# Four modulation chunks of the second layer on GpSimd, and a new order of loads, modulation pieces and start

## Chip, cores and metric

The kernel runs on one core of one Trainium2 chip. The metric is device time in microseconds (us) of one execution, the median of several. All data are float32.

## What is computed

A first block of two layers over 256 tokens of width 2048, and behind it a second block of one layer (two-way scans over tokens and context, then a mixture of 16384 small experts). What this change touches is the input projection of the first block's layers and the second block's modulation:

```python
for i in range(DEPTH):                       # first block, DEPTH = 2
    u = rms_norm(h, norm_g[i]); z = u @ w_in[i]
    ...                                      # three kinds of attention -> mixed
    h = h + mixed @ w_o[i]
    h = h + (p[i] @ w_ple[i]) * jax.nn.sigmoid(h @ w_pg[i])
...
# second block
sh1, sc1, gt1, sh2, sc2, gt2 = split(silu(c) @ w_ada + b_ada, 6)
csh1, csc1, cgt1, ...        = split(silu(c_ctx) @ w_ada + b_ada, 6)
```

Of the modulation of the context only the first two of six parts (shift and scale before its projection) are used. `silu(c) @ w_ada` is a row of 12288 numbers, made in 24 chunks of 512.

## The kernel before

**Weight stream.** All large weights lie in one DRAM tensor `stream` of chunks (2048 x 512), each cut into four pieces: four blocks of 128 rows, laid out as 128 x 2048, 1 MB. SyncE's queue loads the pieces in the fixed order `RING` (made by `layer_order`) into the four buffers of `ring`, round robin; a load waits until the buffer's last piece is used (`piece_used`, L886). To keep float32 precision at TensorE's faster rate, each main piece is split into two: ScalarE rounds it to `high` (`split`, L1846) and VectorE subtracts, `ring - high`, into `ring_r` (L2460). TensorE multiplies with both (`product`, three matmuls of 512 columns, L301 to L303), for two tiles of 128 tokens and four blocks: 24 matmuls a piece (`products`).

**Slots.** A layer has 88 slots, one main piece each: 56 of the input projection, 16 of the output projection, 16 of the gate. After the products of slot q every engine does its share of side work for that slot (`side(l, q)`: norms, rope, heads, attention, turns), so the program order on each engine is written out by hand. In slots 14 to 77 ScalarE and VectorE do side work first and then the split of that slot, elsewhere the split first. Slots 60 and 61 share their products.

**Modulation pieces.** Seven modulation chunks lie in each of the two layers, four pieces each, at the slots listed in `ADA_SLOTS`: the piece follows the main piece of that slot in the ring. It isn't split: TensorE multiplies it directly in float32 with two columns, `silu(c)` and `silu(c_ctx)` (`ada_pe`, L350). After the fourth piece ScalarE copies the four partial rows from PSUM to `mod_rows` (`ada_act`, L366), at the slot after the chunk's last TensorE turns and sums them to columns (`ada_turn`, L357), and VectorE keeps them in `adac` (`ada_dve`, L371).

**Large loads.** GpSimd issues them in its own order, behind waits for their places: `w_uq` and `w_ukv` (L955, L956) once the tiles of `x` are split, the residual (2 MB, L959) when all heads are done, in the second layer then `trig`, `b_ada`, the context in four parts (L964) and `final_g` (L966), then `w_ple` (2 MB) and `pT` (L969, L970) after slot 69. At the end of the second layer it stores the residual in quarters (L979), each behind `gate_used`, which VectorE signals in `use_gate(l, e)` at slot 78 + 4e.

**Beginning.** SyncE loads `cols`, `wtail`, `bc`, `positions`, `inv_freq`, `lam`, then `x` in four parts, then the ring. VectorE makes the rotary angles, ScalarE their sines; TensorE turns `x` (`turn_x`, L1049, L1050), ScalarE rounds it (`round_x`, L1853), VectorE makes the low halves (`split_x`, L2467); then slots 0 to 2 are split and multiplied.

Of the kernel before, what the change touches and what calls it, by code (L numbers as in the profile page):

```python
# [26 lines left out]
ALU = mybir.AluOpType  # L27
# [137 lines left out]
def build_program(nc, t):  # L165
    ctx = ExitStack()
    with ctx:
# [65 lines left out]
        consts = sem("consts")  # L233
# [294 lines left out]
        EXP_FIRST = SIDE_FIRST  # L528

# [342 lines left out]
        def _(sp):  # L872

            sp.dma_start(cols[:, :], t["cols"]).then_inc(consts, 16)
            sp.dma_start(wsmall[:, 0:256], t["wtail"]).then_inc(consts, 16)
            sp.dma_start(bc[:, :], t["bc"].partition_broadcast(P)).then_inc(consts, 16)
# [3 lines left out]
            for e in range(4):  # L880
                sp.dma_start(hx[:, :, e * CHUNK:(e + 1) * CHUNK], t["x"][:, e * CHUNK:(e + 1) * CHUNK].rearrange("(t p) d -> p t d", p=P))\
                  .then_inc(x_loaded[e], 16)
            for c, j, b, u in RING:
                if u >= 1:
                    sp.wait_ge(piece_used[b], u)
                sp.dma_start(ring[:, b, :], t["stream"][c, j]).then_inc(piece_full[b], 16)  # L886
# [52 lines left out]
        def _(pool):  # L939
            for n, (name, l) in enumerate(STAGES):  # L940
# [8 lines left out]
                elif name == "layers":  # L949
                    for l in range(DEPTH):  # L950
# [88 lines left out]
        def _(pe):  # L1039
# [3 lines left out]
            for n, (name, l) in enumerate(STAGES):  # L1043
                begin(pe, n, () if name in FLOWING or name == "peer" else ALL)
                if name == "layers":
# [17 lines left out]
                    def head_groups(l, r):  # L1063

                        if r == 0:
                            pe.wait_ge(turn_read["act"], TURN_ACT(l, "ta", 1))
                            pe.wait_ge(turn_read["dve"], TURN_DVE(l, "ta", 2))
                            pe.wait_ge(layer_loads, 48 * l + 32)
# [141 lines left out]
                    def embed(l, i):  # L1210

                        e, s = i // 2, i % 2
                        if i == 0:
# [7 lines left out]
                    def side(l, q):  # L1221
# [44 lines left out]
                        elif q == 50:  # L1266
# [3 lines left out]
                            pe.wait_ge(ada_done, ADA_LAYER * l + 5)  # L1270
# [72 lines left out]
                    for e in range(4):  # L1343
                        pe.wait_ge(x_loaded[e], 16)
                        turn_x(e, (2 * e, 2 * e + 1))
# [492 lines left out]
        def _(sc):  # L1838
            for n, (name, l) in enumerate(STAGES):
                begin(sc, n, () if name in FLOWING else ALL)  # L1840
                if name == "layers":
# [133 lines left out]
                    def side(l, q):  # L1975
# [110 lines left out]
                        for a0, slots in enumerate(ADA_SLOTS):  # L2086
                            if q == slots[-1] + 2:
                                ada_act(sc, ADA_LAYER * l + a0)

                    sc.wait_ge(consts, 16 * 3)  # L2090
                    sc.activation(cols[:, C_SILU:C_SILU + 2 * KT], cols[:, C_SILU:C_SILU + 2 * KT], ACT.Silu)
                    sc.wait_ge(trig_made, 1)
                    sc.activation(trig[:, 1, :, :], zs[:, 128:192].rearrange("p (t n) -> p t n", t=NT), ACT.Sin)
                    sc.activation(trig[:, 0, :, :], zs[:, 192:256].rearrange("p (t n) -> p t n", t=NT), ACT.Sin)
                    sc.activation(st[:, 64:68], st[:, 68:72], ACT.Exp).then_inc(lam_exp, 1)
                    for e in range(4):
                        round_x(0, e, (2 * e, 2 * e + 1))
                    sc.copy(tail_high, wtail[:, 0]).then_inc(tail_made, 1)
                    for q in range(3):
                        split(0, q)  # L2100
                    for e in range(4):
                        sc.wait_ge(x_loaded[e], 16)
                        square_x(hx, e)
                    sc.drain().then_inc(x_square, 1)
                    for l in range(DEPTH):
                        for q in range(SLOTS):
                            if (l or q >= 3) and q not in EXP_FIRST:
                                split(l, q)
                            if l:
# [326 lines left out]
        def _(dve):  # L2436
# [12 lines left out]
            for n, (name, l) in enumerate(STAGES):  # L2449
# [5 lines left out]
                elif name == "layers":  # L2455
# [196 lines left out]
                    def add_out(l, n4):  # L2652

                        if n4 == 0:
                            dve.wait_ge(layer_loads, 48 * (l + 1))
# [189 lines left out]
                    dve.wait_ge(small, 16 * 3)  # L2845
                    pos, inv = st[:, 80:82], zs[:, 0:32]
                    chain(dve, "dve", dve.tensor_copy(pos, sti[:, 0:NT]))
                    for s in range(NT):
                        a = dve.tensor_scalar(zs[:, 32 + s * 32:64 + s * 32], inv, pos[:, s:s + 1], None, ALU.mult)
                    chain(dve, "dve", a)  # L2850
                    ang, turns, r = zs[:, 32:96], zs[:, 96:160], zs[:, 128:192]
                    turns = zs[:, 256:320]

                    chain(dve, "dve", dve.tensor_scalar(turns, ang, float(np.float32(1 / TWO_PI)), 12582912.0, ALU.mult, ALU.add))
                    chain(dve, "dve", dve.tensor_scalar(turns, turns, 12582912.0, None, ALU.subtract))
                    c1 = 6.28125
                    c2 = float(np.float32(np.round((TWO_PI - c1) * 2 ** 20) / 2 ** 20))
                    c3 = float(np.float32(TWO_PI - c1 - c2))
                    prev = ang
# [788 lines left out]
```

## Time and profile before

| | us |
|---|---|
| median of 3 runs | 3770.86 (3768.49 to 3772.71) |
| profiled execution | 3777.06 |
| its span | 3775.5 |
| TensorE matmul busy | 3712.3 (98%) |
| VectorE busy | 2363.9 (63%) |
| ScalarE busy | 1571.1 (42%) |
| GpSimd busy | 109.2 (3%) |
| mean granted TensorE clock | 0.994 |

The profiled execution is one run with the hardware profiler; its span is the time from the first to the last recorded instruction. Busy shares are averages over the whole span; matmul ends are modelled, so 98% is the share of time with matmuls in flight and not the share of TensorE's peak. Granted clock 1 is the upper level of TensorE's clock. The two layers take the first 1290 us of the span.

### The profile page before, as it was taken

The numbers are of one execution on the slowest core, as the hardware profiler recorded it, in microseconds if no ns is written. First come the engines' busy times: TensorE is split into PE (matmuls) and PEld (weight loads), VectorE is DVE, ScalarE is ACT, GpSimd is POOL, SyncE is SP. The second block draws the span as 40 slices with busy tenths as digits, with TensorE's granted clock in tenths as the row PEclk, the third lists the DMA queues.
The fourth block names the chain that finished last, engine by engine and source line by source line (L and its number), as shares of the span: only waits on it lengthen the run. The fifth ranks groups of instructions, "written<-read, shape, count | busy, mean of one in ns | idle before, by whom it ended". The sixth has DMA issues, their size and how long they took to land.

```text
span 3775.5 us, 48150 instructions
## 1 busy us (share of the span) xinstructions
PE 3712.3 (98%) x20154; PEld 3127.5 (83%) x20154; DVE 2363.9 (63%) x3164; ACT 1571.1 (42%) x1559; POOL 109.2 (3%) x147
## 2 busy tenths in 40 slices
PE   7999999999999999999999999999999999999998
PEld 6777877777777778988888799999988888888886
DVE  4456644436645767665746589777566666667877
ACT  4344535334444521255543433355433333333333
POOL 0000000000000000020000000000000000000000
PEclk9999999999999999999999999999999999999999
DMA  6545565745565467543466445556666666666664
GB/s 247 185 170 221 208 229 189 265 156 206 212 245 211 163 241 283 212 178 126 149 213 258 169 168 191 205 208 235 227 240 228 228 222 222 222 245 234 236 248 173
DMA packets 118857, 799.34 MB, mean 212 GB/s; under 512 B 13264, under 2 KB 13648, under 8 KB 31120
## 3 DMA queue, kind: packets, MB, share of 16 engines
q1 hardware_dynamic: 96992, 692.73, 51.3%
q0 software_dynamic: 19376, 82.96, 5.7%
q10 hardware_dynamic: 2304, 20.97, 1.3%
q8 instruction: 142, 2.33, 0.2%
q14 instruction: 43, 0.35, 0.0%
HBM read 752.57 MB, written 44.04 MB: 211 GB/s over the span
## 4 chain that ended last, share of the span: by engine, by line
PE 91%; DVE 3%; DMA 3%; ACT 2%; POOL 1%; issue 0%; SPq 0%; DVEq 0%; POOLq 0%; ACTq 0%
PE ps L301 25%; PE ps L303 24%; PE ps L302 24%; PE ps L1771 5%; DMA ring<-in_stream_dram 3%; PE ps L1773 2%; PE ps L1723 2%; DVE ring_r L2460 1%; PE ps L350 1%; ACT high L1846 1%; PE ps L1218 1%; PE ps L1082 1%; PE ps L1562 1%; DVE ring_r L315 1%; PE ps L1511 0%; PE ps L1050 0%
## 5 line engine op out<-in xcount | busy, mean ns | idle before, releaser
L309 ACT CAST high<-ring 128x2048 fp32r<-128x2048 f32 x384 | 733.7, 1912 | 1191.9 <-DMA ring<-in_stream_dram 1187.1
L315 DVE TENSOR_TENSOR ring_r<-ring,high 128x2048 fp32r<-128x2048 f32 x384 | 880.1, 2293 | 539.3 <-ACT high L309 537.2
L303 PE MATMUL ps<-high,act_r 128*128 128x512 f32 x1952 | 763.5, 391 | 0.0
L301 PE MATMUL ps<-high,z_r 128*128 128x512 f32 x1728 | 678.9, 393 | 2.8 <-DVE z L3475 1.3
L302 PE MATMUL ps<-ring_r,z_r 128*128 128x512 f32 x1728 | 673.5, 390 | 0.0
L301 PE MATMUL ps<-high,h_r 128*128 128x512 f32 x1600 | 643.7, 402 | 21.4 <-DVE ring_r L2460 17.8
L2460 DVE TENSOR_TENSOR ring_r<-ring,high 128x2048 fp32r<-128x2048 f32 x176 | 402.5, 2291 | 379.8 <-ACT high L1846 378.1
L302 PE MATMUL ps<-ring_r,h_r 128*128 128x512 f32 x1600 | 625.6, 391 | 0.0
L303 PE MATMUL ps<-high,z_r 128*128 128x512 f32 x1376 | 535.9, 389 | 0.0
L302 PE MATMUL ps<-act_r,high 128*128 128x256 f32 x1664 | 471.7, 283 | 0.0
L1846 ACT CAST high<-ring 128x2048 fp32r<-128x2048 f32 x176 | 334.5, 1911 | 279.6 <-DMA ring<-in_stream_dram 278.9
L303 PEld LDWEIGHTS ps<-high,act_r 128*128 128x128 f32 x1952 | 367.9, 188 | 79.3
L301 PE MATMUL ps<-act_r,high 128*128 128x256 f32 x1472 | 420.7, 286 | 2.4 <-DVE act_r L3331 2.4
L303 PE MATMUL ps<-act_r,ring_r 128*128 128x256 f32 x1472 | 417.4, 284 | 0.0
L301 PEld LDWEIGHTS ps<-high,h_r 128*128 128x128 f32 x1600 | 301.3, 188 | 131.7 <-issue 48.6
L301 PEld LDWEIGHTS ps<-high,z_r 128*128 128x128 f32 x1728 | 324.9, 188 | 82.4 <-issue 14.8
L302 PEld LDWEIGHTS ps<-ring_r,z_r 128*128 128x128 f32 x1728 | 325.1, 188 | 67.2 <-issue 1.0
L302 PEld LDWEIGHTS ps<-ring_r,h_r 128*128 128x128 f32 x1600 | 301.6, 189 | 58.2 <-issue 0.7
L302 PEld LDWEIGHTS ps<-act_r,high 128*128 128x128 f32 x1664 | 320.0, 192 | 0.0
L303 PEld LDWEIGHTS ps<-high,z_r 128*128 128x128 f32 x1376 | 258.3, 188 | 54.5
L1771 PE MATMUL ps<-act_r,high 128*128 128x512 f32 x832 | 294.8, 398 | 0.0
L301 PEld LDWEIGHTS ps<-act_r,high 128*128 128x128 f32 x1472 | 283.1, 192 | 2.5 <-issue 2.5
(509 smaller groups left out, 3968.5 us busy)
## 6 DMA issues: line engine op xcount, KB each, us to landing
ring<-in_stream_dram SPq DMA_DIRECT2D x656, 1024.0 KB, 4.8
hidden<-z POOLq DMA_DIRECT2D x32, 512.0 KB, 6.4
gate_matrix<-z ACTq DMA_DIRECT2D x8, 2048.0 KB, 7.0
r<-gate_matrix POOLq DMA_DIRECT2D x32, 512.0 KB, 6.4
z<-hidden POOLq DMA_DIRECT2D x32, 512.0 KB, 6.8
r<-in_w_ple_dram POOLq DMA_DIRECT2D x2, 2048.0 KB, 9.4
merge_gates<-r ACTq DMA_DIRECT2D x8, 512.0 KB, 5.1
r<-merge_gates POOLq DMA_DIRECT2D x4, 1024.0 KB, 5.9
```

Source lines behind the costliest of these rows:

```text
L301: pe.matmul(out, lhs[0], rhs[0], start=start, stop=False)
L302: pe.matmul(out, lhs[0], rhs[1], start=False, stop=False)
L303: return pe.matmul(out, lhs[1], rhs[0], start=False, stop=stop)
L309: sc.copy(high[:, j, :], ring[:, j, :]).then_inc(piece_high[j], 1)
L315: dve.tensor_tensor(ring_r[:, j, :], ring[:, j, :], high[:, j, :], ALU.subtract).then_inc(piece_low[j], 1)
L350: mm = pe.matmul(ps[32 * q:32 * q + 2, 7, :], cols[:, C_SILU + 2 * k:C_SILU + 2 * k + 2], ring[:, b, q * CHUNK:(q + 1) * CHUNK], start=(j ...
L1082: mm = pe.matmul(ps[:, bank, (hd % 2) * TOK:(hd % 2 + 1) * TOK], w[:, k, hd * HD:(hd + 1) * HD], src[:, k, :], start=(k == 0), stop=(k == ...
L1723: mm = pe.matmul(ps[:, 4 + t // 4 % 4, (t % 4) * P:(t % 4 + 1) * P], hot1[:, k % HOTS, t % 8, :], hot2[:, k % HOTS, t % 8, :], start=True, ...
L1771: mm = pe.matmul(ps[:, b, :].rearrange("p (s n) -> p s n", s=2), w[0], halves_2(k), start=(k == 0), stop=(k == KT - 1))
L1773: mm = pe.matmul(ps[:, b, TOK:], w[1], high_2(k), start=False, stop=False)
L1846: sc.copy(high[:, b, :], ring[:, b, :]).then_inc(piece_high[b], 1)
L2460: dve.tensor_tensor(ring_r[:, b, :], ring[:, b, :], high[:, b, :], ALU.subtract).then_inc(piece_low[b], 1)
```

## The change

Four modulation chunks of the second layer (8, 11, 12 and 13, `ADA_POOL`) are multiplied and summed on GpSimd: for each block of 128 rows the 128 x 512 weights times the column `silu(c)`, added to `mod_rows`. The turn on TensorE then also sums over the partitions (a product with a column of ones). Only the token's modulation is made, not the context's. The places of all modulation pieces change. `w_uq` is loaded in three parts, `w_ple` in four, and these and the context's parts stand behind waits for given slots. At the beginning `x` parts and the first pieces alternate in SyncE's queue, the first parts of `x` are processed between the first slots, and angles and squares come in slots 3 to 7.

```diff
-ADA_SLOTS = ((5, 8, 9, 11), (14, 15, 16, 17), (28, 30, 31, 32), (35, 36, 37, 38), (41, 43, 44, 45), (57, 59, 61, 63), (76, 78, 80, 83))
+ADA_SLOTS = ((3, 5, 7, 9), (12, 14, 16, 18), (28, 30, 32, 34), (38, 40, 42, 44), (59, 61, 63, 65), (68, 70, 72, 74), (77, 79, 81, 83))
+ADA_POOL = (8, 11, 12, 13)
...
+        def ada_pool(pool, a, j):
+
+            b, u = A_AT[a, j]
+            if j == 0:
+                pool.wait_ge(ada_turned, a)
+            pool.wait_ge(piece_full[b], 16 * (u + 1))
+            for q in range(PIECE_KT):
+                k = PIECE_KT * j + q
+                w, c = ring[:, b, q * CHUNK:(q + 1) * CHUNK], cols[:, C_SILU + 2 * k:C_SILU + 2 * k + 1]
+                if k == 0:
+                    o = pool.tensor_scalar(mod_rows, w, c, None, ALU.mult)
+                else:
+                    chain(pool, "pool", pool.tensor_scalar(w, w, c, None, ALU.mult))
+                    o = pool.tensor_tensor(mod_rows, mod_rows, w, ALU.add)
+                if q < PIECE_KT - 1:
+                    chain(pool, "pool", o)
+            o.then_inc(piece_used[b], 1)
+            pool.wait_ge(piece_used[b], u + 1)
+            if j == 3:
+                pool.drain().then_inc(ada_rows, 1)
+
...
+            if a in ADA_POOL:
+                pe.wait_ge(ada_done, a)
+                for b in range(4):
+                    mm = pe.matmul(ps[:, 7, 2 * b:2 * b + 1], mod_rows[:, b * P:(b + 1) * P], ones[:, 0:1], start=True, stop=True)
+                mm.then_inc(ada_turned, 1)
+                return
...
+            if a in ADA_POOL:
+                dve.tensor_copy(adac[:, 4 * a:4 * a + 4, 0], ps[:, 7, 0:8:2]).then_inc(ada_done, 1)
+                return
...
+            sp.dma_start(cols[:, :], t["cols"]).then_inc(x_loaded[0], 16)
+            sp.dma_start(wsmall[:, 0:256], t["wtail"]).then_inc(x_loaded[0], 16)
+            load_x(0)
+            load_piece(*RING[0])
+            load_x(1)
+            load_piece(*RING[1])
+            load_x(2)
+            load_piece(*RING[2])
+            load_x(3)
+            load_piece(*RING[3])
...
+            sp.dma_start(bc[:, :], t["bc"].partition_broadcast(P)).then_inc(small, 16)
+            for piece in RING[4:]:
+                load_piece(*piece)
...
-                        pool.dma_start(w_uq, t["w_uq"][l].rearrange("(k p) n -> p k n", p=P)).then_inc(layer_loads, 16)
+                        for k in range(3):
+                            if k:
+                                b, u, _ = W_AT[l, 2 * k]
+                                pool.wait_ge(piece_used[b], u + 1)
+                            pool.dma_start(w_uq[:, k, :], t["w_uq"][l][k * P:(k + 1) * P, :]).then_inc(layer_loads, 16)
+                        b, u, _ = W_AT[l, 6]
+                        pool.wait_ge(piece_used[b], u + 1)
                         pool.dma_start(w_ukv, t["w_ukv"][l].rearrange("(k p) n -> p k n", p=P)).then_inc(layer_loads, 16)
+                        if l + 1 == DEPTH:
+                            for j in range(4):
+                                ada_pool(pool, 8, j)
                         pool.wait_ge(at_out, HEADS * (l + 1))
                         pool.wait_ge(at_done, HEADS * (l + 1))
                         pool.dma_start(hx_of[l], (HRES if l else t["x"]).rearrange("(t p) d -> p t d", p=P)).then_inc(layer_loads, 16)
...
                             pool.dma_start(trig[:, :, :, :], t["trig2"]).then_inc(consts_p, 16)
                             pool.dma_start(b_ada, t["b_ada"]).then_inc(consts_p, 16)
                             for e in range(4):
+                                b, u, _ = W_AT[l, (57, 59, 61, 63)[e]]
+                                pool.wait_ge(piece_used[b], u + 1)
+                                if e:
+                                    ada_pool(pool, 11, e - 1)
                                 pool.dma_start(crows[:, :, e, :], t["ctx"][:, e * CHUNK:(e + 1) * CHUNK].rearrange("(t p) d -> p t d", p=P)).then_inc(consts_p, 16)
+                            ada_pool(pool, 11, 3)
                             pool.wait_ge(tile_full, TILES(l, "mixed", 9))
                             pool.dma_start(final_g, t["final_g"].partition_broadcast(P)).then_inc(aux, 16)
+                            ada_pool(pool, 12, 0)
                         b, u, _ = W_AT[l, OUT_SLOT + OUT_PIECES.index((3, 1))]
                         pool.wait_ge(piece_used[b], u + 1)
-                        pool.dma_start(w_ple, t["w_ple"][l].rearrange("(k p) n -> p k n", p=P)).then_inc(ple_loaded, 16)
                         pool.dma_start(pT, t["pT"][l].rearrange("(k p) n -> p k n", p=P)).then_inc(ple_loaded, 16)
+                        for e in range(4):
+                            cs = slice(e * CHUNK, (e + 1) * CHUNK)
+                            if e:
+                                if l + 1 == DEPTH:
+                                    ada_pool(pool, 12, e)
+                                b, u, _ = W_AT[l, (71, 73, 76)[e - 1]]
+                                pool.wait_ge(piece_used[b], u + 1)
+                                pool.wait_ge(ple_loaded, 80 * l + 16 * (e + 1))
+                            pool.dma_start(w_ple[:, :, cs], t["w_ple"][l][:, cs].rearrange("(k p) n -> p k n", p=P)).then_inc(ple_loaded, 16)
                         if l + 1 < DEPTH:
                             pool.wait_ge(gate_used, 4 * (l + 1))
                             pool.dma_start(HRES.rearrange("(t p) d -> p t d", p=P), hx).then_inc(h_spilled, 16)
                     for e in range(4):
+                        ada_pool(pool, 13, e)
...
-                            pe.wait_ge(ple_loaded, 32 * (l + 1))
-                        else:
+                        if s == 0:
+                            pe.wait_ge(ple_loaded, 80 * l + 32 + 16 * e)
+                        if i:
...
+                    def turn_first_x(e):
+
+                        pe.wait_ge(x_loaded[e], 48 if e == 0 else 16)
+                        if e == 3:
+                            pe.wait_ge(tile_low, TILES(0, "x", 4))
+                        turn_x(e, X_BANKS[e])
+
+                    turn_first_x(0)
+                    turn_first_x(1)
                     for l in range(DEPTH):
                         for q in range(SLOTS):
+                            if l == 0 and q == 3:
+                                pe.wait_ge(tile_low, TILES(0, "x", 8))
                             for p, blocks in parts_of(q):
                                 products(l, p, blocks)
+                            if l == 0 and q < 2:
+                                turn_first_x(2 + q)
...
-                                    elif q == 57:
+                                    elif q == 59:
                                         pe.wait_ge(tile_low, TILES(l, "mixed", 5))
-                                    ada_pe(pe, a, slots.index(q))
+                                    if a not in ADA_POOL:
+                                        ada_pe(pe, a, slots.index(q))
```

ScalarE's and VectorE's orders at the beginning change accordingly: `round_x(0, e)` and `split_x(0, e)` alternate with `split(0, e)`; the squares of `x` come at slots 3 and 4, the angles at slots 4 (VectorE) and 6 (ScalarE); an early `Silu` on `ones` comes ahead of the first wait.

## Rows read from the trace of the kernel before

**Rows 1.** The page's first part: span, busy time and share of each engine, instructions.

```profile
span 3775.5 us, 48150 instructions
...
PE 3712.3 (98%) x20154; PEld 3127.5 (83%) x20154; DVE 2363.9 (63%) x3164; ACT 1571.1 (42%) x1559; POOL 109.2 (3%) x147
```

**Rows 2.** Waits of TensorE, 0 to 1400 us: us in total, times, longest.

```profile
PE ps L301 <- DVE ring_r L2460: 22.7, 19, 9.0
PE ps L1049 <- DMA act<-in_x_dram: 9.4, 1, 9.4
```

**Rows 3.** Stretches: length; PE, PEld, DVE, ACT, POOL busy (instructions); PEclk; DMA share; GB/s.

```profile
23.30:29.80 6.50, 6.42 (x19) 4.68 (x20) 4.90 (x7) 6.28 (x16) 0.00 (x0) 0.54 0.00 0
...
1103.90:1107.90 4.00, 3.99 (x11) 3.14 (x12) 3.59 (x4) 1.25 (x1) 0.00 (x0) 0.57 1.02 429
```

**Rows 4.** Timeline of the beginning: start us, us, engine, line, operation.

```profile
3.81 2.47 SPq L881 DMA_DIRECT2D act<-in_x_dram  x4
...
9.40 0.45 PE L1049 MATMUL ps<-ident,act 128*128 128x128 f32 x1 [9.40 <-DMA act<-in_x_dram]
```

**Rows 5.** The chain of waits, the beginning: start us, us, what.

```profile
19.12 1.81 ACT high L1846
20.95 2.30 DVE ring_r L2460
23.38 0.76 PE ps L301
```

**Rows 6.** The chain of waits: one piece that TensorE waited for, slot 8.

```profile
82.30 4.80 DMA ring<-in_stream_dram
87.12 1.92 ACT high L1846
89.06 2.30 DVE ring_r L2460
```

**Rows 7.** The chain of waits, slots 83 and 84 of the second layer.

```profile
1265.79 0.97 PE ps L350 x8
1266.76 0.43 PE ps L301
...
1272.47 0.79 PE ps L357 x8
```

**Rows 8.** The chain of waits: the piece beside the large loads.

```profile
1087.81 11.71 DMA ring<-in_stream_dram
```

**Rows 9.** Groups of GpSimd's instructions by shape: busy us, mean ns, idle before.

```profile
L388 POOL TENSOR_TENSOR z<-z,trig 128x512 f32<-128x512 f32 x1 | 1.3, 1297 | 0.0
...
L944 POOL TENSOR_SCALAR_AFFINE_SELECT ident<-ident 128x128 f32<-128x128 f32 x1 | 0.3, 295 | 0.2 <-POOL ident L943 0.2
```

**Rows 10.** Timeline of GpSimd, 1640 to 1680 us (the rope of the scan).

```profile
1650.33 2.32 POOL L386 TENSOR_TENSOR act<-z,trig 128x512 f32<-128x512 f32 x1
...
1659.21 1.28 POOL L389 TENSOR_TENSOR act<-z,trig 128x512 f32<-128x512 f32 x1
...
1661.82 3.35 POOL L391 TENSOR_TENSOR z<-act 128x512 f32<-128x512 f32 x1
1665.45 1.29 POOL L386 TENSOR_TENSOR z<-z,trig 128x512 f32<-128x512 f32 x1 [0.29 <-POOL z L391]
```

**Rows 11.** Timeline of VectorE in the same stretch.

```profile
1651.71 3.09 DVE L315 TENSOR_TENSOR ring_r<-ring,high 128x2048 fp32r<-128x2048 f32 x1 [0.21 <-ACT high L309]
...
1661.58 2.43 DVE L315 TENSOR_TENSOR ring_r<-ring,high 128x2048 fp32r<-128x2048 f32 x1
```

**Rows 12.** Timeline of VectorE, 1240 to 1300 us (gate quarters, pieces).

```profile
1246.24 1.29 DVE L2684 TENSOR_TENSOR act<-z 128x512 f32<-128x512 f32 x2
...
1256.50 2.29 DVE L2460 TENSOR_TENSOR ring_r<-ring,high 128x2048 fp32r<-128x2048 f32 x1 [1.66 <-ACT high L1846]
...
1277.37 1.29 DVE L2684 TENSOR_TENSOR act<-z 128x512 f32<-128x512 f32 x2
```

**Rows 13.** Timeline of GpSimd, 1060 to 1300 us: the third store.

```profile
1278.96 0.73 POOL L979 DMA_DIRECT2D residual<-act  x1 [30.39 <-DVE act L2684]
```

More of the change, by code:

```diff
@@ L2086, in side, with angles @@
                         for a0, slots in enumerate(ADA_SLOTS):
-                            if q == slots[-1] + 2:
+                            if q == slots[-1] + 2 and ADA_LAYER * l + a0 not in ADA_POOL:
                                 ada_act(sc, ADA_LAYER * l + a0)
-                    sc.wait_ge(consts, 16 * 3)
+                    sc.activation(rs[:, 90:91], ones[:, 0:1], ACT.Silu)
+                    sc.wait_ge(x_loaded[0], 48)
                     sc.activation(cols[:, C_SILU:C_SILU + 2 * KT], cols[:, C_SILU:C_SILU + 2 * KT], ACT.Silu)
[L2092 to L2095, printed above, removed]
-                    for e in range(4):
[L2097 to L2104, printed above, removed]
+                    def angles():
+                        sc.wait_ge(trig_made, 1)
+                        sc.activation(trig[:, 1, :, :], zs[:, 128:192].rearrange("p (t n) -> p t n", t=NT), ACT.Sin)
+                        sc.activation(trig[:, 0, :, :], zs[:, 192:256].rearrange("p (t n) -> p t n", t=NT), ACT.Sin)
+                        sc.activation(st[:, 64:68], st[:, 68:72], ACT.Exp).then_inc(lam_exp, 1)
+                    for e in range(4):
+                        round_x(0, e, X_BANKS[e])
+                        if e == 0:
+                            sc.copy(tail_high, wtail[:, 0]).then_inc(tail_made, 1)
+                        if e < 3:
+                            split(0, e)
                     for l in range(DEPTH):
@@ L2108, in _ @@
                                 split(l, q)
+                            if l == 0 and q in (3, 4):
+                                for e in (2 * q - 6, 2 * q - 5):
+                                    sc.wait_ge(x_loaded[e], 48 if e == 0 else 16)
+                                    square_x(hx, e)
+                                if q == 4:
+                                    sc.drain().then_inc(x_square, 1)
+                            elif l == 0 and q == 6:
+                                angles()
                             if l:
@@ L2844, in _ @@
                     dve.tensor_reduce(sel16[:, :], ident[:, :].rearrange("p (q s) -> p s q", q=4)[:, 0:16, :], AX_X, ALU.add)
[L2845 to L2858, printed above, removed]
@@ L2859, in _ @@
-                    prev = ang
-                    for cc in (c1, c2, c3):
-                        chain(dve, "dve", dve.scalar_tensor_tensor(r, turns, -cc, prev, ALU.mult, ALU.add))
-                        prev = r
-                    pi = float(np.nextafter(np.float32(np.pi), np.float32(0)))
-                    chain(dve, "dve", dve.tensor_scalar(r, r, pi, -pi, ALU.min, ALU.max))
-                    c = zs[:, 192:256]
-                    chain(dve, "dve", dve.scalar_tensor_tensor(c, r, -1.0, r, ALU.mult, ALU.max))
@@ L2886, in _, with angles @@
-                    chain(dve, "dve", dve.tensor_tensor(st[:, 60:62], e[:, :, 1], e[:, :, 0], ALU.subtract))
-                    for ly in range(DEPTH):
-                        init = 0.8 - 0.6 * float(np.exp(-0.3 * ly))
-                        dve.tensor_scalar(st[:, 60 + ly:61 + ly], st[:, 60 + ly:61 + ly], -init, None, ALU.add)
-                        dve.tensor_scalar(bc[:, B_SUB + ly * HD:][:, 0:HD], bc[:, B_SUB + ly * HD:][:, 0:HD], 1.0 - init, None, ALU.mult)
+                    def angles():
+                        dve.wait_ge(small, 16 * 4)
+                        pos, inv = st[:, 80:82], zs[:, 0:32]
+                        chain(dve, "dve", dve.tensor_copy(pos, sti[:, 0:NT]))
+                        for s in range(NT):
+                            a = dve.tensor_scalar(zs[:, 32 + s * 32:64 + s * 32], inv, pos[:, s:s + 1], None, ALU.mult)
+                        chain(dve, "dve", a)
+                        ang, turns, r = zs[:, 32:96], zs[:, 96:160], zs[:, 128:192]
+                        turns = zs[:, 256:320]
+                        chain(dve, "dve", dve.tensor_scalar(turns, ang, float(np.float32(1 / TWO_PI)), 12582912.0, ALU.mult, ALU.add))
+                        chain(dve, "dve", dve.tensor_scalar(turns, turns, 12582912.0, None, ALU.subtract))
+                        c1 = 6.28125
+                        c2 = float(np.float32(np.round((TWO_PI - c1) * 2 ** 20) / 2 ** 20))
+                        c3 = float(np.float32(TWO_PI - c1 - c2))
+                        prev = ang
+                        for cc in (c1, c2, c3):
+                            chain(dve, "dve", dve.scalar_tensor_tensor(r, turns, -cc, prev, ALU.mult, ALU.add))
+                            prev = r
+                        pi = float(np.nextafter(np.float32(np.pi), np.float32(0)))
+                        chain(dve, "dve", dve.tensor_scalar(r, r, pi, -pi, ALU.min, ALU.max))
+                        c = zs[:, 192:256]
+                        chain(dve, "dve", dve.scalar_tensor_tensor(c, r, -1.0, r, ALU.mult, ALU.max))
+                        dve.tensor_scalar(c, c, -1.0, float(np.float32(np.pi / 2)), ALU.mult, ALU.add)
+                        lam = zs[:, 512:1024].rearrange("p (k l n) -> p k l n", k=4, l=DEPTH)
+                        for ly in range(DEPTH):
+                            for pr in range(2):
+                                k = 2 * ly + pr
+                                dve.tensor_tensor_reduce(zs[:, 1024 + k * 64:][:, 0:64], lam[:, 2 * pr, ly, :], lam[:, 2 * pr + 1, ly, :],
+                                                         1.0, 0.0, ALU.mult, ALU.add, st[:, 68 + k:69 + k])
+                        dve.drain().then_inc(trig_made, 1)
@@ new lines, in factors @@
+                    def factors():
+                        dve.wait_ge(lam_exp, 1)
+                        e = st[:, 64:68].rearrange("p (l k) -> p l k", k=2)
+                        chain(dve, "dve", dve.tensor_tensor(st[:, 60:62], e[:, :, 1], e[:, :, 0], ALU.subtract))
+                        for ly in range(DEPTH):
+                            init = 0.8 - 0.6 * float(np.exp(-0.3 * ly))
+                            dve.tensor_scalar(st[:, 60 + ly:61 + ly], st[:, 60 + ly:61 + ly], -init, None, ALU.add)
+                            dve.tensor_scalar(bc[:, B_SUB + ly * HD:][:, 0:HD], bc[:, B_SUB + ly * HD:][:, 0:HD], 1.0 - init, None, ALU.mult)
@@ L2891, in _ @@
+                    dve.wait_ge(x_loaded[0], 48)
+                    for e in range(4):
+                        split_x(0, e, X_BANKS[e])
+                        if e == 0:
+                            dve.wait_ge(tail_made, 1)
+                            dve.tensor_tensor(tail_low, wtail[:, 0], tail_high, ALU.subtract).then_inc(tail_made, 1)
+                        if e < 3:
+                            split(0, e)
                     for l in range(DEPTH):
@@ L2894, in _ @@
                                 split(l, q)
+                            if l == 0 and q == 4:
+                                angles()
+                            elif l == 0 and q == 7:
+                                factors()
                             if l:
```

47 lines of the change are left out of this document (12 added, 35 removed).

## Prediction

> **What bounds the kernel now.** I read the page's first part first: TensorE is busy for 98% of the span [rows 1], so time comes only out of TensorE's own work or out of its idle time, and anything that another engine does matters only when TensorE ends up waiting for it. Next the waits of TensorE over the two layers [rows 2]. The reader is to see that there is little to win by better timing: 9.4 us for the first part of `x`, and 22.7 us for the halves of weight pieces, of which one wait at the start is 9.0 and the other eighteen share 13.7. Then the stretches right behind an idle time [rows 3]: after the 9.0 us wait the granted clock is 0.54 for 6.5 us, and after a wait of 3.0 us it is 0.57 for 4.0 us. Those are the lower of TensorE's two levels, and they cost 3.0 us and 1.7 us beside the waits themselves. Last, the chain of waits, which shows what a late piece goes through: load 4.80, cast on ScalarE 1.92, subtraction on VectorE 2.30 [rows 6], 9.1 us with the hand-overs, of which TensorE then makes 24 products in about 5.5 us (from 1266.76 to 1272.47 at slot 84, less the slow first product [rows 7]).
>
> The SyncE queue issues the pieces strictly in ring order, four buffers deep. A piece of slot q is called Mq here, a modulation piece that follows it Aq. With modulation pieces at every second slot the buffer of Aq is next used by M(q+3), since M(q+1), M(q+2) and A(q+2) lie between. So M(q+3) is ready 9.1 us after Aq is used, and TensorE wants it when M(q+2) is finished.
>
> **Gains.** (1) *Start.* `x` is issued behind six small or broadcast loads and its first part lands at 9.40, 5.6 us after the issue at 3.81 [rows 4]. Four parts of it are then turned and rounded before the first piece is cast at 19.12, subtracted until 23.25 and multiplied from 23.38 [rows 5]. In the changed kernel the first part of `x` is third in the queue (issue about 1.9, landing about 7.0 to 7.5). ScalarE rounds one part (four operations, 1.5 us), casts the piece to 12, VectorE subtracts to 14.3: the first product starts 9.1 us earlier. Two parts are turned between slots 0 to 2 instead of in the idle time, 16 transposes of 0.11 us, 1.8 us in all. The later slots have their halves in time by the same reckoning (slot 3's at about 37 against a start at 38), and the angles and squares fall into slots 3 to 7, behind pieces already loaded. Net 7.3, between 5 and 10. (2) *Sixteen pieces off TensorE.* Each takes 0.97 us, and the product behind it 0.43 where 0.23 is usual [rows 7]: 16 x 1.17 = 18.7 us (15.5 without the second part). The turn of each chunk stays (0.79 us). (3) *Places.* The clusters with modulation pieces at adjoining slots leave less than 9.1 us; most of the 13.7 us lies there and behind large loads. Every second slot leaves two main pieces and one modulation piece, 11.9 us. I take 8 (3 to 12), clock losses included. (4) *Large loads in parts.* The 3.0 us wait comes after a piece that took 11.71 us to land [rows 8], beside the residual and context loads. The 2 MB residual load is still issued whole just ahead. I take 3 (0 to 6). Gains: 7.3 + 18.7 + 8 + 3 = 37; bounds 24 and 47.
>
> **What a piece costs on GpSimd.** There are four multiplications by a scalar and four additions, 128x512 each, every one chained to the last. A two-input operation of that form takes 1.30 us undisturbed [rows 9]. The one-input form is not in the trace: by scaling the selection of 128x128 with its fixed part taken as a 0.2 us memset's it is about 0.57, and it will not cost more than the two-input form's 1.30. I take 0.7, near the one-input row. With about 0.1 us for each chained wait: 4 x 1.30 + 4 x 0.7 + 0.8 = 8.8 us; a chunk's first piece has one addition less, 7.3 us with its missing wait. Bounds alone are 8.0 and 11.
>
> Alone it is not. While VectorE subtracts a 128x2048 piece, GpSimd's 1.3 us operations take 2.32 to 3.35 us; the later one began 0.24 us behind VectorE's 2.43 us subtraction and lasted 2.06 us beyond its usual time [rows 10, 11]. So GpSimd stands still for nearly the whole of such a subtraction, and VectorE loses little: 3.09 for 2.29 at worst. In a stretch where TensorE finishes two main pieces there are two subtractions, 4 us: 12.8 us for a piece, 11.2 for a first one (one subtraction and the gating products of slot 59). Bounds are 8.0 (no overlap) and 16.
>
> The Trainium skill speaks against this move: "GPSIMD Engine Reference", section Engine selection, keeps elementwise work on VectorE, puts two-input operations on GpSimd at about twice the time and one-input ones near line rate, and its Key points say that GpSimd shares its SBUF interfaces with VectorE when that has two SBUF inputs. The trace agrees on the sharing. At line rate for the one-input operations (an estimate from the page: 512 columns at 1.2 GHz, 0.43 us) a piece would take 7.7 us alone instead of 8.8, and the sum below would be some 5 us better.
>
> **What holds the pieces up.** *Chunk 8* (slots 12 to 18). GpSimd can start a piece as it lands, and slots 14 to 17 also carry the query and key products of the heads, so M15, M17, M19 and M21 have over 12 us to spare for A. Nothing. *Chunk 11* (59 to 65). GpSimd waits until TensorE has used M59 before it starts A59, and M61 before A61, M63 before A63 (the order written there serves the context loads). Take M59's end as 0. A59 is done at 11.2, M62 ready at 20.3; TensorE is through M60 and M61 at 12.1: a stall of 8.2, and 3 us at the low clock. A61 runs 12.8 to 25.6, M64 is ready at 34.7 against 34.3: 0.4. A63 starts at M63's end and is done at 47.8, M66 ready at 56.9 against 46.5: 10.4, and 3 of clock. Together 25; with pieces of 8.0 it is 13, with 16 it is 31. A65 then just suffices for the turn at slot 66. *Chunk 12* (68 to 74). A70 starts 1.5 us behind M69's end (two DMA issues), so M73 is ready at 1.5 + 12.8 + 9.1 = 23.4 against 17.3: 6.1, and 3 of clock, 9; bounds 1 and 12. *Chunk 13* (77 to 83). Each piece stands behind the wait and the store for a quarter of the residual. The second quarter is released by VectorE at 1247.5, the third at 1278.7, when the store is issued (1278.96) [rows 12, 13]. So A81 runs from 1248.3 to 1261.1, M84 is ready at 1270.2 against 1265.8: 4.4. M84's subtraction ended at 1258.8 before [rows 12]; 11 us later, with M85 and M86 and the third quarter behind it in VectorE's order, that quarter comes some 7 us later. A83 cannot start before 1286 and ends at 1295 (VectorE now waits too, so 8.8). But TensorE wants the whole chunk at slot 84's end, where its turn is at 1272.47 [rows 7]: it comes 22.6 us late. Clock 3. Together 26 (4.4 is inside the 22.6); with 8.0 us and M84 in time 1279.3 + 8.0 - 1272.5 + 3 = 18; upper 30. What is late next is the key and value stage, which starts that much later: it is bound by TensorE itself and gives nothing back.
>
> **Sum.** Losses 25 + 9 + 26 = 60 (bounds 32 and 73), gains 37 (24 and 47): 23 us slower. The profiled execution took 3777.06 (span 3775.5 and 1.6 around it), 6.2 above the median of the three runs, so from it the changed kernel takes 3800; the same difference on the median gives 3770.9 + 23 = 3794 us.
>
> **Rivals.** *A, the pieces are cheap* (the other side): if the subtractions don't hold GpSimd and a piece takes about 8, losses are 32 and gains 37 to 47: 3756 to 3766. Point of decision: losses under 30. For it speaks that most of rows 10 in the second rope half run at 1.29; against it the waits at M59, M63 and the third quarter, which stand however short a piece is. *B, hidden and paid back*: losses about equal to gains, pieces near 9.5, within 7.5 us of 3771. *C, contention above my value*: in the first rope half six operations took 14.8 us instead of 7.8, a factor of 1.9. At 16 us a piece losses are 73 and the time is 3771 + 36 = 3807, with the smallest gains 3820. *D, the start does not move*, because the loads are limited by bandwidth: 3801, inside the range. *E*, only the last turn stalls and chunks 11 and 12 run free (if my reading of their waits is wrong): 26 against 37, 3760.
>
> **Chances.** Forecast with C and D 0.68 (slower), B 0.13 (same), A and E 0.19 (faster); 0.2% is 7.5 us, about what this kernel's measurement can tell from nothing. The range runs from 3758 (A and E's better half left out) to 3816 (C's worst left out); the forecast's own is 3780 to 3812.
>
> **What the profile would show.** First product near 14.3; 320 instead of 448 records for line 350's matmuls; GpSimd some 200 us busier, its additions 1.3 or 3.3; TensorE waits of 6 to 10 us for M62, M66 and M73, and one of about 16 at the turn behind slot 84, released by GpSimd, each followed by a stretch at the low clock. I am wrong if GpSimd's pieces are finished before TensorE has used the two main pieces behind them, or if the third quarter is released much earlier than slot 84's end.

## The result

The changed kernel takes 3825.1 us in the median (3821.5 to 3827.2, 4 runs) against 3771.8 for the kernel before beside it: a ratio of 1.0141, 95% interval 1.0128 to 1.0155, so 53 us slower. The direction was forecast, the size was not: 3794 was predicted and 3816 was the end of the range.

The profile after, first part and shares of the chain that ended last. The line numbers have moved (L1846 is now L1925, L2460 is L2548, L1049 is L1117, L1218 is L1286, L357 is L380 for the chunks on GpSimd).

```profile
span 3820.0 us, 48041 instructions
...
PE 3701.5 (97%) x20026; PEld 3131.0 (82%) x20026; DVE 2382.0 (62%) x3164; ACT 1565.8 (41%) x1546; POOL 338.9 (9%) x281
...
PE 88%; POOL 4%; DVE 3%; DMA 2%; ACT 1%; issue 1%; POOLq 0%; DVEq 0%; SPq 0%; ACTq 0%
```

TensorE is busy for 11 us less than in [rows 1] and the span is 44.5 us longer; GpSimd is 230 us busier and now has a share of the chain. The waits of TensorE, 0 to 1500 us (total, times, longest), answer to [rows 2]:

```profile
PE ps L301 <- DVE ring_r L2548: 44.1, 17, 9.3
PE ps L380 <- POOLq L373: 21.0, 3, 20.1
PE ps L1286 <- ACT z L2139: 12.7, 1, 12.7
PE ps L1117 <- DMA act<-in_x_dram: 8.3, 2, 6.6
```

All long ones but the 6.6 us for the first part of `x` lie behind the heads of the second layer. The beginning, by contrast, did what it should. In its timeline the first part of `x` is there at 6.57 and the first product comes at 13.84, 9.5 us before that of [rows 5]:

```profile
6.57 0.45 PE L1117 MATMUL ps<-ident,act 128*128 128x128 f32 x1 [6.57 <-DMA act<-in_x_dram]
...
13.84 0.77 PE L301 MATMUL ps<-high,h_r 128*128 128x512 f32 x1 [1.59 <-DVE ring_r L2548]
```

GpSimd's groups by shape (busy us, mean ns, idle before) show the price that [rows 9] did not hold:

```profile
L366 POOL TENSOR_SCALAR ring<-ring,cols 128x512 f32<-128x512 f32 x60 | 119.4, 1991 | 19.0 <-DMA ring<-in_stream_dram 9.5 <-PE ps L303 4.4
L367 POOL TENSOR_TENSOR wsmall<-wsmall,ring 128x512 f32<-128x512 f32 x60 | 95.2, 1587 | 5.0
```

The one-input multiplication is dearer than the two-input addition. Undisturbed it is 1.56 against 1.26 to 1.30, as the timeline of GpSimd for A61 shows, and beside VectorE's subtractions 3.48:

```profile
1088.96 1.56 POOL L366 TENSOR_SCALAR ring<-ring,cols 128x512 f32<-128x512 f32 x1 [0.34 <-PE ps L303]
1090.60 1.26 POOL L367 TENSOR_TENSOR wsmall<-wsmall,ring 128x512 f32<-128x512 f32 x1
...
1094.96 3.48 POOL L366 TENSOR_SCALAR ring<-ring,cols 128x512 f32<-128x512 f32 x1
...
1099.90 3.48 POOL L366 TENSOR_SCALAR ring<-ring,cols 128x512 f32<-128x512 f32 x1
1103.46 1.29 POOL L367 TENSOR_TENSOR wsmall<-wsmall,ring 128x512 f32<-128x512 f32 x1
```

A61 begins 0.34 us behind TensorE's use of M61 and ends at 1104.75 (1103.46 + 1.29), after 15.8 us. VectorE's own rows in that stretch are the subtractions of M62 and M63:

```profile
1094.32 2.69 DVE L2548 TENSOR_TENSOR ring_r<-ring,high 128x2048 fp32r<-128x2048 f32 x1 [13.99 <-ACT high L1925]
1098.64 3.30 DVE L2548 TENSOR_TENSOR ring_r<-ring,high 128x2048 fp32r<-128x2048 f32 x1 [1.63 <-ACT high L1925]
```

And this is what TensorE did meanwhile, M62, M64 and M66 in its timeline of chunk 11, and M73 in chunk 12:

```profile
1097.15 0.77 PE L301 MATMUL ps<-high,z_r 128*128 128x512 f32 x1 [8.31 <-DVE ring_r L2548]
...
1113.91 0.77 PE L301 MATMUL ps<-high,r_r 128*128 128x512 f32 x1 [4.18 <-DVE ring_r L2548]
...
1134.58 0.80 PE L301 MATMUL ps<-high,z_r 128*128 128x512 f32 x1 [7.08 <-DVE ring_r L2548]
```

```profile
1188.69 0.76 PE L301 MATMUL ps<-high,h_r 128*128 128x512 f32 x1 [9.31 <-DVE ring_r L2548]
```

The last chunk holds the largest losses. First GpSimd (second store, A81, third store, A83), which answers to [rows 13]:

```profile
1266.21 0.78 POOL L1047 DMA_DIRECT2D residual<-act  x1 [13.79 <-DVE act L2772]
1267.04 2.25 POOL L366 TENSOR_SCALAR ring<-ring,cols 128x512 f32<-128x512 f32 x1
...
1279.28 1.26 POOL L367 TENSOR_TENSOR wsmall<-wsmall,ring 128x512 f32<-128x512 f32 x1
1304.72 0.77 POOL L1047 DMA_DIRECT2D residual<-act  x1 [24.18 <-DVE act L2772]
1305.53 1.57 POOL L366 TENSOR_SCALAR ring<-ring,cols 128x512 f32<-128x512 f32 x1
...
1316.20 1.26 POOL L367 TENSOR_TENSOR wsmall<-wsmall,ring 128x512 f32<-128x512 f32 x1
```

Then ScalarE and TensorE in the same stretch:

```profile
1285.27 1.90 ACT L1925 CAST high<-ring 128x2048 fp32r<-128x2048 f32 x1 [20.98 <-DMA ring<-in_stream_dram]
1287.07 0.58 ACT L2139 COPY z<-ps 128x512 f32<-128x512 f32 x1
```

```profile
1287.70 3.76 PE L1286 MATMUL ps<-r 128*128 128x512 f32 x4 [12.70 <-ACT z L2139]
...
1317.91 1.87 PE L380 MATMUL ps<-ones,wsmall 128*128 128x1 f32 x8 [20.09 <-POOLq L373]
```

ScalarE's program has the cast of M84 ahead of the copy of an embedding product. M84's load waits for A81, so ScalarE sits 21 us, and TensorE, which needs that copy's bank already at slot 83, stops there for 12.7 us. The wait that names ScalarE is GpSimd's. Behind it comes the forecast one: A83 stands behind the third store, and the turn behind slot 84 waits 20.1 us. Two stretches (columns as in [rows 3]) show the lower level of the clock behind that wait, 0.54, and the mean over the 270 us from the heads to the last turn, 0.87:

```profile
1318.00:1326.00 8.00, 8.00 (x24) 6.65 (x25) 0.39 (x2) 1.90 (x1) 0.60 (x1) 0.54 0.72 281
```

```profile
1060.00:1330.00 270.00, 199.45 (x827) 155.26 (x826) 121.75 (x107) 90.98 (x100) 179.34 (x109) 0.87 0.50 193
```

### The profile page after: what moved, and what is told of

The parts are those of the page before. It is cut to its first block, busy times and chain, and to the rows that moved or that the text cites. A ratio compares the mean times of both kernels' runs of the same rounds, so it can differ in the third digit from the quotient of the medians.

```text
span 3820.0 us, 48041 instructions
## 1 busy us (share of the span) xinstructions
PE 3701.5 (97%) x20026; PEld 3131.0 (82%) x20026; DVE 2382.0 (62%) x3164; ACT 1565.8 (41%) x1546; POOL 338.9 (9%) x281
## 4 chain that ended last, share of the span: by engine, by line
PE 88%; POOL 4%; DVE 3%; DMA 2%; ACT 1%; issue 1%; POOLq 0%; DVEq 0%; SPq 0%; ACTq 0%
PE ps L301 24%; PE ps L303 23%; PE ps L302 23%; PE ps L1850 5%; PE ps L1852 2%; DMA ring<-in_stream_dram 2%; POOL ring L366 2%; PE ps L1802 1%; POOL wsmall L367 1%; PE ps L350 1%; DVE ring_r L2548 1%; PE ps L1150 1%; PE ps L1641 1%; DVE ring_r L315 1%; ACT high L1925 0%
## 5 line engine op out<-in xcount | busy, mean ns | idle before, releaser
L2548 DVE TENSOR_TENSOR ring_r<-ring,high 128x2048 fp32r<-128x2048 f32 x176 | 409.5, 2327 | 382.4 <-ACT high L1925 381.1
L1925 ACT CAST high<-ring 128x2048 fp32r<-128x2048 f32 x176 | 335.3, 1910 | 336.1 <-DMA ring<-in_stream_dram 335.2
```

The source lines that it names most:

```text
L1925: sc.copy(high[:, b, :], ring[:, b, :]).then_inc(piece_high[b], 1)
L2548: dve.tensor_tensor(ring_r[:, b, :], ring[:, b, :], high[:, b, :], ALU.subtract).then_inc(piece_low[b], 1)
```

## Experiments

(In the kernels here line numbers are up to 3 higher or lower than in the changed one.) All runs compare with the kernel before on the same chip; its median was 3772.2 to 3773.0. The 95% intervals are 4 to 6 us to either side, so a difference of less than some 5 us between two kernels is not clear of noise. "Theory 1" is that GpSimd's long pieces hold the ring's buffers, "theory 2" that GpSimd costs in proportion to its busy time, "theory 3" that the new places or beginning carry part of the loss.

**Which part loses.** `ADA_POOL` sets which chunks GpSimd makes; a chunk that is not in it goes back to TensorE at its new place.

```diff
-ADA_POOL = (8, 11, 12, 13)
+ADA_POOL = ()             # pool_none;  (8,) pool_8;  (8, 11) pool_8_11;  (8, 13) pool_8_13;  (8, 12) pool_8_12
         def ada_pool(pool, a, j):
             b, u = A_AT[a, j]
+            if a not in ADA_POOL:
+                return
```

No chunk on GpSimd. 

> The changed kernel with no chunk on GpSimd: all four go back to TensorE, at their new places; beginning, places and parts of loads as changed. Theory 1 (the loss is the ring held up by GpSimd's pieces of about 16 us, and the rest of the change is the gain I took it for: 7 at the start, 8 by places, 3 by loads): 3754 us. Theory 2 (GpSimd's work costs in proportion to its busy time, by slowing VectorE, wherever it lies): the same 3754. Theory 3 (the new places or the new beginning carry part of the loss): 3772 or more.

Measured 3759.3 us, ratio 0.9963 (0.9949 to 0.9977). Theory 3 falls: the rest of the change gains 13 us. It is 5 less than the 18 expected, but the interval (9 to 19 us) holds the 18 too.

Chunk 8 alone. 

> As above, but chunk 8 (slots 12 to 18, beside the heads' projections) on GpSimd. Theory 1: hidden, four pieces off TensorE at 1.17 us, 5 us faster than without any: 3749. Theory 2: a quarter of the whole loss of some 71 us: 3771.

Measured 3754.6, ratio 0.9954 (0.9937 to 0.9970), the fastest kernel here. The medians differ by 4.7 from the run above, the four pieces' worth that was forecast (4 x 1.17), though the two intervals overlap. Theory 2 falls: four pieces of 13.3 to 15.0 us on GpSimd, from 719 to 786 us, cost nothing visible. Around them TensorE is busy without a gap at the upper clock (1.00), in this run (first line) as in the one with nothing on GpSimd (second line; columns as in [rows 3]):

```profile
700.00:850.00 150.00, 150.00 (x697) 119.66 (x698) 74.34 (x118) 59.65 (x81) 54.74 (x31) 1.00 0.48 178
700.00:850.00 150.00, 150.00 (x709) 116.07 (x709) 65.90 (x109) 58.92 (x80) 0.00 (x0) 1.00 0.49 178
```

Chunks 8 and 11. 

> Chunks 8 and 11 on GpSimd. Theory 1: the waits of TensorE in chunk 11 of the changed kernel (8.3 + 1.5 + 4.2 + 7.1 = 21 us) and some 8 us of low clock, less 5 for the pieces: 24 us slower than with chunk 8 alone, 3773. Theory 2: as for every chunk, about 18 slower.

Measured 3775.0, ratio 1.0010 (1.0001 to 1.0020): 20.4 us above chunk 8 alone. This run by itself doesn't part theory 1 (24) from theory 2 (18).

Chunks 8 and 13. 

> Chunks 8 and 13 on GpSimd. Theory 1: the waits 2.9 + 12.7 + 20.1 = 36 us of the changed kernel and some 8 us of low clock, less 5: 39 us slower than with chunk 8 alone, 3788; a few less if the lateness of A77 came from chunk 12. Theory 2: about 18 slower, 3767 to 3789.

Measured 3790.8, ratio 1.0048 (1.0032 to 1.0065): 36.2 above. The chunks cost very different amounts for the same work. Its waits are the same two as in the changed kernel, so they belong to chunk 13 and not to what came before it:

```profile
PE ps L382 <- POOLq L375: 21.1, 1, 21.1
PE ps L301 <- DVE ring_r L2550: 12.9, 13, 2.4
PE ps L1288 <- ACT z L2141: 12.4, 1, 12.4
```

Chunks 8 and 12. 

> Chunks 8 and 12 on GpSimd. If the chunks' costs add up, chunk 12 costs what is left of the changed kernel's loss: 3825 - 3755 - 20 (chunk 11) - 36 (chunk 13) = 14, so 3769. If the three in a row make each other worse: less, 3762 to 3766.

Measured 3764.7, ratio 0.9973 (0.9963 to 0.9983): 10.1 above chunk 8 alone, in the second range. The three chunks singly add 20.4 + 10.1 + 36.2 = 66.7 and together 70.5, so nearly all of the loss is the sum of the single ones. The 4 us that are left are within the noise; whether standing in a row adds anything is not settled.

**When a piece starts.** In the next two, pieces are moved ahead of the waits that stand before them in GpSimd's order.

```diff
                     for e in range(4):
                         ada_pool(pool, 13, e)
+                    for e in range(4):
                         if e == 3:
```

> Chunks 8 and 13 on GpSimd as in the run before, but all four pieces of chunk 13 ahead of the residual's stores in GpSimd's order, so that none waits for a gate quarter. Theory 1 (the start behind those waits is what delays them): the pieces follow each other from slot 76's end, 15 to 16 us each; M82 and M84 are late by 2 us each at most, the turn at slot 84 by 0 to 2: 3753 to 3758, so 33 to 38 faster than with the waits (3791). Theory 4 (the pieces are too long for their places wherever they start): three further pieces behind a first, each 16 against 14.5 us of TensorE's work between them, and the low clock: 3765 or more.

Measured 3756.5, ratio 0.9960 (0.9946 to 0.9974): 34.3 us faster than with the waits, and 1.9 above chunk 8 alone. The same work, 15.4 us a piece here, now costs almost nothing, so theory 4 falls for this chunk. Its waits from 1180 to 1290 us, where there had been 36:

```profile
PE ps L301 <- DVE ring_r L2551: 4.1, 3, 1.4
PE ps L382 <- POOLq L375: 1.5, 1, 1.5
```

```diff
                             for e in range(4):
+                                if e:
+                                    ada_pool(pool, 11, e - 1)
                                 b, u, _ = W_AT[l, (57, 59, 61, 63)[e]]
                                 pool.wait_ge(piece_used[b], u + 1)
-                                if e:
-                                    ada_pool(pool, 11, e - 1)
```

> Chunks 8 and 11 on GpSimd, but each piece of chunk 11 ahead of the wait for its slot (the context's loads still wait). Theory 1: A59 then starts about 10 us earlier, but pieces of 16 us come every 12 us of TensorE's work, so that GpSimd itself is the limit: waits of about 2, 5 and 4 us instead of 8.3, 4 and 8: 3766, against 3775 with the waits. Theory 4: the wait for the slot costs nothing, 3775.

Measured 3763.3, ratio 0.9973 (0.9963 to 0.9983): 11.7 us faster than with the waits, 8.7 above chunk 8 alone. Theory 4 falls. GpSimd now works on the four pieces from 1066.2 to 1131.3 us with no gap above 0.3 us, 16.3 us a piece, and is the limit itself, as expected. TensorE's waits that are left are 1.9 us for M60, 1.0 for M62 and 5.9 for M66; expected were 2, 5 and 4 for M62, M64 and M66.

All four chunks on GpSimd, with both of these edits. 

> The changed kernel with the pieces of chunk 11 ahead of the waits for their slots and those of chunk 13 ahead of the stores; chunk 12 as changed. By the sum of the single ones: 3755 with chunk 8 alone, 8 for chunk 11 early, 2 for chunk 13 early, 14 for chunk 12: 3779. If GpSimd's queue of pieces grows over three chunks in a row, each 16 us against 12 to 14 of TensorE's work: up to 3790.

Measured 3779.6, ratio 1.0020 (1.0010 to 1.0030): 45.5 us faster than the changed kernel, as the sum said. It is still 25 above chunk 8 alone.

**How long a piece is.** Here part of the computation is left out of the pieces.

```diff
-                    chain(pool, "pool", pool.tensor_scalar(w, w, c, None, ALU.mult))
                     o = pool.tensor_tensor(mod_rows, mod_rows, w, ALU.add)
```

> Chunks 8 and 11 on GpSimd with the waits as they were, but the multiplications by the scalar left out of every block but a chunk's first (the modulation is then wrong in these chunks): a piece has four additions, 5.6 us alone and 7 to 9 beside VectorE. Theory 1: M62 late by 2 to 4 us, M64 in time, M66 late by 4 to 6, 3 of clock: 3761 to 3765, against 3775 with pieces of 16 us and 3755 with chunk 11 on TensorE. Theory 4': only the start behind the slot matters, not the length: 3770 or more.

Measured 3761.7, ratio 0.9973 (0.9964 to 0.9983): 13.3 us faster than with the multiplications, 7 above chunk 8 alone. So the length matters, and theory 4' falls. The time is in the expected range, but its parts are not the expected ones, and the agreement is in part luck: M62 was 1.7 us late, M64 5.2 instead of in time, and M66 in time instead of 4 to 6 late. With M62 nearly in time, TensorE is through M63 12.9 us behind M61's end, instead of 21.9 in the run with the multiplications, and even a piece of 8.7 us that starts only behind M61 holds M64 up. The chain of waits shows it:

```profile
1100.41 1.30 POOL wsmall L368
1101.73 4.84 DMA ring<-in_stream_dram
1106.60 1.91 ACT high L1926
1108.53 2.30 DVE ring_r L2549
1110.96 0.77 PE ps L301
```

Length and start both matter.

The last one sets the length near to what the prediction had assumed, in the changed kernel with all four chunks:

```diff
-                    chain(pool, "pool", pool.tensor_scalar(w, w, c, None, ALU.mult))
+                    chain(pool, "pool", pool.tensor_scalar(w[:, 0:256], w[:, 0:256], c, None, ALU.mult))
```

> The changed kernel, all four chunks on GpSimd, but each multiplication over 256 of the 512 columns (the other half of the block goes into the sum unscaled): about 0.8 us where the trace showed 1.56, so a piece takes 9 us alone, what the prediction assumed. Theory 1 with the price of the one-input operation as the step that failed: the loss falls to what the prediction summed, 3794, and at most 8 more for TensorE's low clock and the late start of A81: 3790 to 3802. Rival (the price was a side matter; the order of waits and the clock make up the difference): 3810 or more.

Measured 3803.6, ratio 1.0079 (1.0062 to 1.0095): 21.5 us faster than the changed kernel, but in neither range: 1.6 above the upper end of theory 1's and 6.4 below the rival's. The multiplication took 0.92 us undisturbed, so a piece alone takes 9.5 us. By the means over all pieces it is about 12.6 us (four of each operation and 0.6 of hand-overs), close to the 12.8 of the sum:

```profile
L367 POOL TENSOR_TENSOR wsmall<-wsmall,ring 128x512 f32<-128x512 f32 x60 | 90.3, 1505 | 5.0
L366 POOL TENSOR_SCALAR ring<-ring,cols 128x256 f32<-128x256 f32 x60 | 89.1, 1485 | 28.7 <-DMA ring<-in_stream_dram 16.7 <-PE ps L303 6.8
```

TensorE's waits, 0 to 1420 us:

```profile
PE ps L301 <- DVE ring_r L2548: 35.1, 17, 6.9
PE ps L380 <- POOLq L373: 17.6, 1, 17.6
PE ps L1117 <- DMA act<-in_x_dram: 8.6, 2, 6.7
PE ps L1286 <- ACT z L2139: 6.5, 1, 6.5
```

**The places by themselves.** `ADA_SLOTS` as before, nothing on GpSimd, beginning and loads as changed.

```diff
-ADA_SLOTS = ((3, 5, 7, 9), (12, 14, 16, 18), ...
+ADA_SLOTS = ((5, 8, 9, 11), (14, 15, 16, 17), ...
```

Two of TensorE's waits that belong to these places go back with them.

> No chunk on GpSimd and the modulation pieces at their old places; beginning and parts of loads as changed. If the places are worth 8 us as I took them: 3767; if the gain is nearly all the beginning (7) and the loads (3) and the places give only 3: 3762; if the places are worth nothing: 3759 as with the new ones.

Measured 3762.4, ratio 0.9975 (0.9966 to 0.9985). The medians put the places at 3 us and beginning with loads at 10.6, though the intervals of this run and the first overlap. The waits for halves of pieces up to 1420 us do fall with the new places, from 16.0 us here to 8.5 there, and the spans of the two profiled executions are 5.6 us apart (3763.3 and 3757.7). The worth of the places is therefore known only as some us.

## Why the prediction missed

*Bound and ring: right.* The losses lie where they were forecast: chunk 8 hidden, chunks 11 and 12 by M62, M66 and M73, chunk 13 by M84 and the turn at slot 84. Line 350 has 320 records instead of 448. The waits at M62 (8.3 against 8.2) and M66 (7.1 against 10.4) were near; M64's was 4.2 against 0.4, M73's 9.3 against 6.1. With 4.7 us added for the four pieces that leave TensorE, chunk 11 lost 25.1 us where 25 had been summed, chunk 12 14.8 where 9 had been, chunk 13 40.9 where 26 had been. Chunk 11's agreement is luck: A59 took 13.3 us instead of 11.2, but TensorE took 14.9 for M60 and M61 instead of 12.1, and M64's wait was too small in the sum by about what M66's was too large.

*The price of a piece: the step that failed.* "... it will not cost more than the two-input form's 1.30. I take 0.7". It costs 1.56 alone. A scale from a 128-column operation of another kind carried no information on the slope; here 256 columns take 0.92 and 512 take 1.56, so 2.5 ns a column with 0.28 fixed. (These two numbers are a line through two points.) So a piece alone takes about 12 us: A83 ran from 1305.53 to 1317.46 (1316.20 + 1.26), 11.9 us. The sum had 8.8, and its upper bound 11 was passed as well. Beside VectorE, the later pieces of chunks 11 to 13 took 13.5 to 16.6 us where 12.8 was taken, the first ones 11.9 to 14.9 where 11.2 was taken. The half multiplication gives the size of this mistake: 21.5 of the 31 us that the forecast was short. What is left there is 30.7 us over the kernel before on the same chip, against a forecast of 23. The 7.7 between them are about the 5 us that the gains were short and the 3 by which the waits in that run (50.6) exceed those summed (47.7); neither is clear of noise by itself.

*Contention: right, and rival C is not what happened.* GpSimd's operations last 2 us longer where they meet a subtraction (3.48 against 1.56). By the means in the changed kernel (1.99 and 1.59) that is 3 us a piece on average, where 4 had been taken. Rival C, the nearest by its number (3807, at most 3820), had pieces of 16 us by a stronger contention; their length came about by the price instead. VectorE loses little: its subtractions of the layers average 2327 ns against 2290 with nothing on GpSimd, 6.5 us over 176 of them. With chunk 8 alone this costs no wait.

*Chunk 13: right mechanism, too small.* It cost 36.2 us net where 26 less 4.7 had been summed. I placed A81 by the time at which the second quarter was released before (1247.5), 15.5 us ahead of M83's end. But that quarter is behind M82's subtraction in VectorE's order, and M82 waits for A79, so it moved too: it came 9.4 us ahead of M83's end, and the wait that M84's lateness caused was 12.7 us where 4.4 had been summed. And TensorE was stopped at slot 83 already, through ScalarE's copy. Moving the pieces ahead of the stores shows that the cause was the start: 34 of the 36 us are gone.

*Gains: 13 instead of 18, not clear of noise.* The beginning gave its part (first product 9.5 us earlier, less 1.8 for the turns); the places gave 3 where 8 was taken, by the medians. The waits for halves of pieces are 8.5 us with the new places and nothing on GpSimd, so more than half of the 13.7 us of before stays. With the pieces of chunk 8 the gain is 17.6 against 22.7.

*The clock: a little short.* From the issue of the residual's load in the second layer to the last store it is 285.6 us in the changed kernel and 215.4 with chunk 8 alone, 70.2 more. The waits there are 70.6 against 2.1, the twelve pieces that TensorE no longer multiplies give 14 back, and 16 us are left, where 12 had been summed for the clock's lower level. They lie in TensorE's own instructions, waits taken out: the same products of the weight pieces take 188.2 us of this stretch against 177.4, although twelve of them no longer follow a modulation piece (2.4 us); the embedding products take 14.7 against 12.6, the turns 3.6 against 2.5. That all of this is clock fits the lower granted clock behind the waits, but no run tests it by itself.

The Trainium skill's page "GPSIMD Engine Reference", section Engine selection, puts one-input operations on GpSimd near line rate and two-input ones at about twice VectorE's time. This trace does not agree on the first: 1.56 us for 512 columns is slower than the two-input form beside it, and 3.6 times the 0.43 us that the prediction estimated from the page. On the second it agrees: 1.26 to 1.30 us against 0.65 on VectorE for the same shape (two in 1.29, [rows 12]). On the sharing of SBUF interfaces with VectorE (its Key points) it agrees too: 1.56 us becomes 3.48 beside a subtraction with two SBUF inputs.

## What to carry to other kernels

Work that is moved to an idle engine is hidden only if it is finished within the time that its buffer may be kept; count from the moment its buffer is next needed, back over load and conversions. Put such work in the idle engine's order ahead of waits that it does not need: that alone was worth 34 us in one chunk. Even so, all four chunks with both early starts (3779.6) stay behind none at all (3759.3); only chunk 8, whose pieces had time to spare, was worth moving, and its 4.7 us are at the edge of the noise. Where the trace has no row for an operation, neither its nearest neighbour nor a kind that ought to be slower bounds it: here 0.7 was taken, 1.30 was held to be the most, and it was 1.56. Measure such an operation alone first. And when a piece is late, re-time every release that stands behind it in another engine's order before adding the next.

## What was not expected of the hardware

GpSimd multiplies 128x512 by a column in 1.56 us and adds two such blocks in 1.29: the operation with one streamed input is the slower one. And TensorE's granted clock over the 270 us with six waits of 4 to 20 us is 0.87, against 1.00 over the same part of the kernel with nothing on GpSimd.
